# Norm factors moved from a matmul's input to its results, in the second attention and the gate/up stage of a two-block transformer kernel

## What is computed

```python
def rms_norm(x, w):
    return x * rsqrt(mean(x * x, axis=-1) + 1e-6) * w

x = rms_norm(x + gate * y, final_norm_g)          # end of the first block
h = rms_norm(x, norm_mix_2)                       # second block
x = x + sliding_window_attention(h, swa_w_in_2, sinks, swa_w_out_2)
h = rms_norm(x, norm_ffn_2)
x = x + (silu(h @ w_gate) * (h @ w_up)) @ w_down
out = rms_norm(x, final_norm_2)
```

## Time and profile before

| | us |
|---|---|
| median of 3 runs | 2732.42 |
| their range | 2731.32 to 2732.61 |
| the profiled execution, its own time | 2737.62 |
| its span, first to last instruction | 2735.8 |
| PE busy | 2568.2 (94%) |
| DVE busy | 1742.0 (64%) |
| ACT busy | 992.6 (36%) |

### The profile page before, as it was taken

One profiled execution on the slowest core, in us unless ns is written; L12 is line 12 of the kernel. 1 busy time (PEld: TensorE's weight loads), 2 busy tenths in 40 slices (PEclk: granted clock), 3 DMA queues, 4 the chain that ended last, 5 costly groups with the idle time before them and its releaser, 6 DMA issues.

```text
span 2735.8 us, 35374 instructions
## 1 busy us (share of the span) xinstructions
PE 2568.2 (94%) x11936; PEld 2138.8 (78%) x11936; DVE 1742.0 (64%) x3025; ACT 992.6 (36%) x1343; POOL 1018.3 (37%) x776
## 2 busy tenths in 40 slices
PE   7999799988899999999999999999998998899998
PEld 5777578676688778778888899999995755688786
DVE  4878977876688888852222487878786385422334
ACT  2222573342333333334444333333333254333322
POOL 0334924333037777787500266667630000000000
PEclk8999899999999999999999999999998979999999
DMA  5221732444224444434544699999992201232221
GB/s 214 77 85 54 273 105 92 146 145 163 85 85 146 138 132 141 137 123 142 208 142 148 213 350 336 351 338 355 336 346 76 93 1 47 69 100 92 98 94 62
DMA packets 177217, 433.54 MB, mean 158 GB/s; under 512 B 32752, under 2 KB 81904, under 8 KB 176752
## 3 DMA queue, kind: packets, MB, share of 16 engines
q1 hardware_dynamic: 123888, 331.61, 35.5%
q0 software_dynamic: 34816, 67.41, 7.0%
q10 hardware_dynamic: 18432, 33.56, 3.3%
HBM read 371.48 MB, written 61.01 MB: 158 GB/s over the span
## 4 chain that ended last, share of the span: by engine, by line
PE 66%; DVE 16%; issue 10%; POOL 6%; ACT 1%; DMA 1%; ACTq 0%; DVEq 0%; POOLq 0%
PE ps L444 13%; PE ps L446 13%; PE ps L445 13%; PE ps L711 8%; PE ps L712 8%; PE ps L713 8%; DVE ar L1280 2%; POOL wlo L1850 2%; POOL ar L1867 2%; DVE wlo L1194 2%; POOL ar L1864 2%; DVE ar L1238 2%; PE ps L467 1%; DVE ar L1631 1%; DVE ar L1633 1%
## 5 line engine op out<-in xcount | busy, mean ns | idle before, releaser
L1194 DVE TENSOR_TENSOR wlo<-raw,whi 128x1024 fp32r<-128x1024 f32 x358 | 438.3, 1224 | 625.3 <-ACT whi L827 623.7
L827 ACT ACTIVATE whi<-raw 128x1024 fp32r<-128x1024 f32 x426 | 451.3, 1059 | 690.3 <-PE ps L713 405.4
L444 PE MATMUL ps<-b_hi,whi 128*128 128x512 f32 x1344 | 537.5, 400 | 29.7 <-DVE wlo L1194 17.3
L445 PE MATMUL ps<-b_lo,whi 128*128 128x512 f32 x1344 | 528.1, 393 | 0.0
L446 PE MATMUL ps<-b_hi,wlo 128*128 128x512 f32 x1344 | 527.8, 393 | 0.0
L1884 POOL DMA_INDIRECT w_scratch<-ar x384 | 427.0, 1112 | 231.0 <-issue 116.7
L444 PE MATMUL ps<-a_hi,whi 128*128 128x512 f32 x832 | 338.3, 407 | 37.9 <-DVE a_lo L1215 22.6
L711 PE MATMUL ps<-a_hi,whi 128*128 128x384 f32 x1024 | 345.3, 337 | 12.3 <-DVE a_lo L1672 12.3
L713 PE MATMUL ps<-a_hi,wlo 128*128 128x384 f32 x1024 | 344.2, 336 | 0.0
L712 PE MATMUL ps<-a_lo,whi 128*128 128x384 f32 x1024 | 344.2, 336 | 0.0
L444 PEld LDWEIGHTS ps<-b_hi,whi 128*128 128x128 f32 x1344 | 255.0, 190 | 99.5 <-DVE wlo L1194 29.0
(11 more groups left out here) (231 smaller groups left out, 3523.7 us busy)
## 6 DMA issues: line engine op xcount, KB each, us to landing
raw<-panels SPq DMA_DIRECT2D x430, 512.0 KB, 3.3
gelu_scratch<-ar ACTq DMA_DIRECT2D x128, 256.0 KB, 2.0
w_scratch<-rstd SPq DMA_DIRECT2D x32, 768.0 KB, 10.9
ar<-w_scratch SPq DMA_DIRECT2D x128, 192.0 KB, 4.5
ar<-gelu_scratch SPq DMA_DIRECT2D x128, 192.0 KB, 5.3
ar<-mod SPq DMA_DIRECT2D x32, 512.0 KB, 4.6
ar<-panels SPq DMA_DIRECT2D x3, 2048.0 KB, 16.5
w_scratch<-ar POOLq DMA_INDIRECT x384
```

The costliest lines, as they stand in the source:

```text
L444: pe.matmul(bank, w_h, hi[:, k, :], start=(k == 0), stop=False)
L445: pe.matmul(bank, w_h, lo[:, k, :], start=False, stop=False)
L827: act.activation(whi[:, u % SPLIT, :], raw[:, u % RAW, :], ACT.Copy).then_inc(hi_ready, 1)
L1194: dve.tensor_tensor(wlo[:, u % SPLIT, :], raw[:, u % RAW, :], f32(whi[:, u % SPLIT, :]), ALU.subtract).then_inc(lo_ready, 1)
```

## The change

The factor of a token multiplies a whole column of a panel's input, so it can as well multiply the same column of the result. The change does that for SW and GU. The input of the matmul becomes `x` times a gain only, and the results are multiplied by `rstd` when they leave PSUM.

- **One factor for two norms.** With r1 the factor of the final norm and g its gain, the two norms give x g r1 r2 times the second gain, and r1 r2 = 1/root(mean(x^2 (g^2 + eps)) + eps^2). So the statistics of the SW input are made of x times root(g^2 + eps) (`root3`), and its gain is the product of the two (`gain3`). DVE makes the two products of 8 columns and ACT the root of one, ahead of the first input of EV.
- **Place A.** DVE alternates the residual add of tile k and the remainder of tile k - 1 (`scaled_lo`); ACT writes `a_hi` straight from `x` and squares the tile; PE puts each tile's statistic behind the tile's three products in the first panel. To make this possible the last EV input goes to slot 7 of `a_hi` (`z_slot`), so that slots 0 to 6 are free earlier, and the four banks are taken in the order 0, 2, 3, 1 (`SWB`), with the statistics in bank 1. The factor r1 alone is still needed for the residual: its 8 statistics (group 4) stand on PE behind the fourth panel in bank 6, root and reciprocal go to `rstd1`, and `x` is multiplied in the shadow of the query panels.
- **Place B.** During SO, ACT writes `a_hi` and DVE `a_lo` of each finished tile of `x`. The first GU panel needs no factor; the last statistic stands behind it. In the loop DVE multiplies each gate bank by `rstd` into `nt`, ACT takes the Silu from there, DVE multiplies each up bank by `rstd` into `hid` and then by the Silu. The first pass of four panels is written out ahead of the loop.

The diff, cut:

```diff
+SWB = (0, 2, 3, 1)
...
+        gain3, root3 = gs1, gs1c
+        def z_slot(n):
+            return KT - 1 if n == NK - 1 else n % 4
...
+                    if k == KT - 1:
+                        last.then_inc(used, 1)
+                    if each:
+                        each(k)
...
-            pe.wait_ge(y_done, 5)
-            norm_stats(3)
-            norm_stats(4)
...
+            pe.wait_ge(y_done, 2)
             for u in range(4):
-                panel(SW + u, u, ps[:, u, :], a_hi, a_lo, r_of(SW) + u + 1, (h_ready, 3 * KT) if u == 0 else None)
+                first = u == 0
+                panel(SW + u, u, ps[:, SWB[u], :], a_hi, a_lo, r_of(SW) + u + 1, (h_ready, 3 * KT) if first else None,
+                      (lambda k: norm_stat(3, k, bank=1)) if first else None)
+                if u == 2:
+                    pe.wait_ge(rt_ready, 4)
+            norm_stats(4, bank=6)
...
-            norm_stat(5, KT - 1)
-            strips(GU, 2 * FT, a_hi, a_lo, ready=(h_ready, 4 * KT))
+            def last_stat(i, u):
+                if isinstance(i, int) and u == 0:
+                    norm_stat(5, KT - 1)
+            strips(GU, 2 * FT, a_hi, a_lo, last_stat, (h_ready, 4 * KT))
...
+            act.wait_ge(fold_g, 2)
+            act.activation(root3[:, :], root3[:, :], ACT.Sqrt, bias=EPS).then_inc(fold_s, 1)
...
-            norm_sq(3, x, made=y_done)
-            norm_sq(4, x, made=y1_ready)
-            norm_hi(3, a_hi, lambda k: col("zero"))
-            only_panels(SW, 12)
+            act.wait_ge(fold_s, 1)
+            for k in range(KT):
+                act.wait_ge(y_done, k + 1)
+                act.wait_ge(used, SW if k == KT - 1 else SW - 1)
+                act.activation(a_hi[:, k, :], x[:, k, :], ACT.Copy, scale=gain3[:, k:k + 1]).then_inc(nhi_ready, 1)
+                if k >= 2:
+                    act.wait_ge(sq_used, 3 * KT + k - 1)
+                act.activation(sq[:, k % 2, :], x[:, k, :], ACT.Square, scale=root3[:, k:k + 1]).then_inc(sq_ready, 1)
+            hi_next(0, SW, 0)
+            act.wait_ge(sq_used, 4 * KT)
+            act.activation(rstd[:, :], ps[:, 1, :], ACT.Sqrt, bias=EPS * EPS, scale=1.0 / D).then_inc(rt_ready, 1)
+            for u in range(1, 4):
+                hi_next(0, SW, u)
+            for k in range(KT):
+                norm_sq_tile(4, k, x)
+            act.wait_ge(sq_used, 5 * KT)
+            act.activation(rstd1, ps[:, 6, :], ACT.Sqrt, bias=EPS, scale=1.0 / D).then_inc(rt_ready, 1)
+            only_panels(SW + 4, 8)
...
-            panels_and_squares(SO, 5, KT)
-            norm_hi(4, a_hi, lambda k: col("zero"))
-            with act.Fori(0, 2 * FT // 4) as i:
+            def wide_hi(k):
+                act.wait_ge(x_ready, KT + k + 1)
+                act.activation(a_hi[:, k, :], x[:, k, :], ACT.Copy, scale=col("ffn", k)).then_inc(nhi_ready, 1)
+                norm_sq_tile(5, k, x)
+            for k in range(KT):
+                hi_next(k // 4, SO, k % 4)
+                if k:
+                    wide_hi(k - 1)
+            wide_hi(KT - 1)
+            def gate_up(i, first=False):
                 for u in range(4):
-                    step(i, GU, u)
+                    hi_next(i, GU, u)
+                    if first and u == 0:
+                        act.wait_ge(sq_used, 6 * KT)
+                        act.activation(rstd[:, :], ps[:, 4, :], ACT.Sqrt, bias=EPS, scale=1.0 / D).then_inc(rt_ready, 1)
                     if u % 2 == 0:
-                        act.activation(sq[:, u // 2, :], ps[:, u, :], ACT.Silu).then_inc(gate_ready, 1)
+                        act.wait_ge(gs_ready, i * 2 + (u // 2 + 1))
+                        if not first:
+                            act.wait_ge(act_done, i * 2 + (u // 2 - 1))
+                        act.activation(sq[:, u // 2, :], nt[:, u // 2, :], ACT.Silu).then_inc(gate_ready, 1)
+            gate_up(0, True)
+            with act.Fori(1, 2 * FT // 4) as i:
+                gate_up(i)
...
+            def scaled_lo(m, k, gain):
+                dve.wait_ge(nhi_ready, m * KT + k + 1)
+                dve.scalar_tensor_tensor(a_lo[:, k, :], x[:, k, :], gain, f32(a_hi[:, k, :]), ALU.mult, ALU.subtract).then_inc(h_ready, 1)
             for k in range(KT):
                 await_bank(k, 0, SW)
                 dve.scalar_tensor_tensor(x[:, k, :], ps[:, k, :], mod[:, 5 * KT + k, 0:1], x[:, k, :], ALU.mult, ALU.add).then_inc(y_done, 1)
+                if k:
+                    scaled_lo(3, k - 1, gain3[:, k - 1:k])
+            scaled_lo(3, KT - 1, gain3[:, KT - 1:KT])
+            lo_next(0, SW, 0)
             norm_rstd(3)
-            dve.wait_ge(y_done, KT)
-            for k in range(KT):
-                dve.scalar_tensor_tensor(x[:, k, :], x[:, k, :], col("final1", k), rstd[:, :], ALU.mult, ALU.mult).then_inc(y1_ready, 1)
-            norm_rstd(4)
-            norm_apply(3, x, lambda k: col("mix", k), lambda k: col("zero"), a_hi, a_lo)
-            for u in range(4):
+            for u in range(1, 4):
                 lo_next(0, SW, u)
-            for u in range(2):
-                dve.wait_ge(used, SW + u + 1)
-                dve.tensor_copy(k2[:, u, :], ps[:, u, :]).then_inc(bank_free, 1)
+                if u == 1:
+                    dve.wait_ge(used, SW + 1)
+                    dve.tensor_tensor(k2[:, 0, :], ps[:, SWB[0], :], rstd[:, :], ALU.mult).then_inc(bank_free, 1)
+                if u == 2:
+                    dve.wait_ge(used, SW + 2)
+                    dve.tensor_tensor(k2[:, 1, :], ps[:, SWB[1], :], rstd[:, :], ALU.mult).then_inc(bank_free, 1)
             for u in range(2):
                 dve.wait_ge(used, SW + u + 3)
-                dve.tensor_copy(v2_feat_sb[:, u, :], ps[:, 2 + u, :]).then_inc(v2_feat, 1)
+                dve.tensor_tensor(v2_feat_sb[:, u, :], ps[:, SWB[2 + u], :], rstd[:, :], ALU.mult).then_inc(v2_feat, 1)
             dve.wait_ge(v2_feat, 2)
             dve.sem_inc(bank_free, 2)
+            lo_next(1, SW, 0)
+            norm_rstd(4, rstd1)
             for u in range(2):
                 dve.wait_ge(v2_turned, u + 1)
                 dve.tensor_copy(v2[:, :, u * P:(u + 1) * P], ps[:, 4 + u, :].rearrange("p (s n) -> p s n", n=P)).then_inc(v2_done, 1)
-            with dve.Fori(0, 2) as i:
-                for u in range(4):
-                    step(i, SW + 4, u)
-                    dve.tensor_scalar(q2[:, bass.ds(i * 4 + u, 1), :], ps[:, u, :], HD2 ** -0.5, None, ALU.mult).then_inc(bank_free, 1)
+            for n in range(8):
+                if n:
+                    lo_next(0, SW + 4, n)
+                dve.wait_ge(used, SW + 4 + n + 1)
+                dve.scalar_tensor_tensor(q2[:, n, :], ps[:, SWB[n % 4], :], HD2 ** -0.5, rstd[:, :], ALU.mult, ALU.mult).then_inc(bank_free, 1)
+                dve.scalar_tensor_tensor(x[:, n, :], x[:, n, :], col("final1", n), rstd1, ALU.mult, ALU.mult).then_inc(y1_ready, 1)
...
-            add_to_x(SO, KT, None, KT, step)
-            norm_rstd(5)
-            norm_apply(4, x, lambda k: col("ffn", k), lambda k: col("zero"), a_hi, a_lo)
-            with dve.Fori(0, 2 * FT // 4) as i:
+            dve.wait_ge(y1_ready, KT)
+            for k in range(KT):
+                step(k // 4, SO, k % 4)
+                dve.tensor_tensor(x[:, k, :], ps[:, k % 4, :], x[:, k, :], ALU.add).then_inc(x_ready, 1)
+                dve.wait_ge(x_ready, KT + k + 1)
+                dve.sem_inc(bank_free, 1)
+                if k:
+                    scaled_lo(4, k - 1, col("ffn", k - 1))
+            scaled_lo(4, KT - 1, col("ffn", KT - 1))
+            def gate_up(i, first=False):
                 for u in range(4):
-                    step(i, GU, u)
-                    if u % 2:
-                        p = i * 2 + u // 2
+                    p = i * 2 + u // 2
+                    lo_next(i, GU, u)
+                    if first and u == 0:
+                        norm_rstd(5)
+                    dve.wait_ge(used, i * 4 + (GU + u + 1))
+                    if u % 2 == 0:
+                        if not first:
+                            dve.wait_ge(gate_ready, p + (2 * KT - 1))
+                        dve.tensor_tensor(nt[:, u // 2, :], ps[:, u, :], rstd[:, :], ALU.mult).then_inc(gs_ready, 1)
+                        dve.wait_ge(gs_ready, p + 1)
+                        dve.sem_inc(bank_free, 1)
+                    else:
+                        at = slice(p, p + 1) if isinstance(p, int) else bass.ds(p, 1)
+                        dve.tensor_tensor(hid[:, at, :], ps[:, u, :], rstd[:, :], ALU.mult).then_inc(up_ready, 1)
+                        dve.wait_ge(up_ready, p + 1)
+                        dve.sem_inc(bank_free, 1)
                         dve.wait_ge(gate_ready, p + (2 * KT + 1))
-                        dve.tensor_tensor(hid[:, bass.ds(p, 1), :], sq[:, u // 2, :], ps[:, u, :], ALU.mult).then_inc(act_done, 1)
-                        dve.wait_ge(act_done, p + 1)
```

(5 more changed lines are left out.)

44 lines of the change are left out of this document (26 added, 18 removed).

## The result

The changed kernel takes **2697.34 us** (median of 4 executions, 2690.37 to 2704.23) beside 2731.87 for the kernel before (4 executions, 2727.89 to 2732.61). The ratio is 0.9876, with a 95% interval of 0.9849 to 0.9904: faster by 34.5 us, a small gain (1.2%) but clear of no change. The forecast was 2702.6, the range 2694 to 2713.

What follows compares the result with a forecast made beforehand. The kernel was taken as a row of matmul stages on PE (66% of the chain), losing time where PE waits. Terms of -22.4, -14.6, +2.5, +0.8, +1.5, +1.6 and +0.8 sum to -29.8 us: 2702.6 us, range 2694 to 2713.

Steps and rivals of the forecast that it cites:

- Part 1: Place A, first panel: 1.54 us a tile with PE slowest; panel 2 starts near 2093.7 instead of 2122.89, -29.2 us.
- Part 2: Rest of place A: the residual's statistics cost PE 7.7 us unhidden, value transposes 0.66; place A in all -22.4 us.
- Parts 3 and 4: Place B: second gate/up panel 14.6 us earlier, wait of +2.5 before the third; loop unchanged, its end +0.8.
- Part 5: Ahead of the expert stage: table load of 1.28 us and root of about 0.2 on PE's path, +1.5 us.
- rival (d): A table load costs a drain of about 1.38 us on top, one wait 1.4 longer: 2704.0 us; chance 0.04.
- Part 6: Half-rate clock after PE's waits: +1.6 us at the expert stage, +0.8 (half a dip) at the third gate/up panel.
- (a): Place A, first panel: add, copy and remainder don't overlap, 2.21 us a tile, 5.3 more: 2707.9 us; chance 0.07.
- (b): Place A runs at half rate, its 8 tiles cost 12.3 us more: 2714.9 us; chance 0.08.
- (c): Gate/up loop becomes bound by the relay PE, DVE, ACT, DVE: slower, 2738 us at a 7.06 relay; chance 0.03.
- (e): Merged norm shortens nothing, since weights or free banks hold the panel: under 0.2% change, 2730 us; chance 0.02.

Runs made afterwards that it cites:

- e4: Changed kernel with the third gate/up panel's weights split ahead of the factor's root and reciprocal: 2693.73 us, ratio 0.9863 to the kernel before.
- e8: Changed kernel with four more DVE passes between a gate panel's end and its Silu: 3090.89 us, in a slower set of runs.

## Why the prediction was right, and by how much it missed

The mechanism was right at both places; -29.8 was expected. The profiles differ by -33.4, of which the attention stage's -3.9 goes with its clock, and -29.5 is left. In order of its parts:

| Part | predicted | trace |
|---|---|---|
| 1. place A, first panel | -29.2 | -29.4 |
| 1 to 2. place A in all | -22.4 | -22.7 |
| 3. place B, first panel | -14.6 | -14.5 |
| 3. wait ahead of the third panel | +2.5 | +2.2 |
| 4. gate/up loop, and its end | 0, +0.8 | 0, +0.9 |
| 5. root and load ahead of the expert stage | +1.5 | +1.4 |
| 6. clock, expert stage | +1.6 | +1.6 here, but not the change's |
| 6. clock, third gate/up panel | +0.8 | +1.6 here; in 4 of 7 profiles |

**Part 1.** A tile takes 1.55 (2084.91 to 2086.46), predicted 1.54; panel 2 starts at 2096.60, which is 26.3 earlier in spite of 3.1 lost ahead. The durations were right as well. The groups of ACT in the changed kernel (count, busy us, mean ns, idle before), with the plain square first:

```profile
L860 ACT ACTIVATE sq<-x 128x512 f32<-128x512 f32 x24 | 14.9, 625 | 16.5 <-PE ps L479 10.7 <-DVE x L1919 5.7
...
L1146 ACT ACTIVATE sq<-x,gs1c 128x512 f32<-128x512 f32 x8 | 5.8, 719 | 1.4 <-PE ps L479 1.4
...
L1143 ACT ACTIVATE a_hi<-x,gs 128x512 fp32r<-128x512 f32 x8 | 5.7, 708 | 2.0 <-DVE x L1775 2.0
```

A square with a column as its scale takes 719 ns against 625: 94 more, as the two rows had it. ACT's idle behind PE in this panel is 1.4 us in all, so PE is the slowest of the three, by the thin margin foreseen.

**Part 2.** The second statistics took 7.25, not 7.7: this term was mis-sized by 0.45, since in the earlier trace rows they also waited for DVE's adds, and here the input is all there. The transposes took 0.88 instead of 0.66, which was a reading too short: the row of 0.66 in the earlier trace rows holds the last four of the eight. With the 0.2 of the first panel and 0.1 more in panels 2 to 4 it comes to -22.7 against -22.4.

**Parts 3 and 4.** The first gate/up panel, its last statistic and the second panel stand as laid out. The wait of 2.18 was 0.3 shorter than the sum of its hand-offs. The end of the loop, PE of the changed kernel, beside the earlier trace rows:

```profile
2561.31 0.77 PE L724 MATMUL ps<-b_hi,whi 128*128 128x512 f32 x1 [3.29 <-DVE b_lo L1907]
```

3.29 instead of 2.46: +0.83, and the half rate that follows stood there before. The remaining 0.1 lies in the landmarks.

**Part 5, and rival (d).** The rows of the start of EV above show the load (1.28), the root right behind it at 1532.04 and the input at 1532.15: no drain. e4 shows the same where ACT was busy up to the load: copy to 2312.01, load at 2312.02, root at 2313.32. The wait grew by 1.38, and load and root together take 1.41 (1530.74 to 1532.15). The Trainium skill (ScalarE: Activation LUTs, What ACT_TABLE_LOAD costs) counts about 1.38 us of drain to every switch. This trace doesn't have it; with it the wait would have grown by some 2.8 (an estimate from that figure).

**Part 6.** This is the step that failed in its reason. The wait of 2.58 was taken for one without a dip, because one profile had none; five of six profiles have one. The kernel before pays it too. In the first two sets, the result's among them, the changed kernel is charged nothing new; in the later sets its dip is longer and costs about 1.1 us more than that of the kernel before. So of the 1.6 us that the forecast books here between 0 and 1.1 are the change's, an error on the pessimistic side. The other 0.8, half of a dip at the third gate/up panel, agrees with four dips in seven, but the kernel before has one in three at its own wait of 1.88, so that the difference is nearer 0.4. That the profile of the kernel before had neither dip was luck, and it is why the sum of the parts fits these two profiles so well.

**The rest.** In medians the change gave 34.5 us, in the forecast 29.8: 4.7 apart. Up to 1.6 of it is the first dip of part 6. The remaining 3.1 lie within the interval of the measurement (26 to 41 us of gain) and are open. A part can be the attention stage, whose mean with the new place A was 1.6 lower, and which the forecast put at nothing.

The rivals: (a) and (b) are refuted by 1.55 us a tile at a clock of 1.00, (c) by the loop that is full from 2333 to 2557 and by e8, (d) by the rows of the load, (e) by the time.
